# RMS norms of a four-layer trunk: the root and the reciprocal move to 128x2 values with the token on the partition, and TensorE spreads them over PSUM

## The reference, cut to what matters

```python
def rms_norm(x, g):
    x32 = x.astype(jnp.float32)
    y = x32 * lax.rsqrt(jnp.mean(x32 * x32, axis=-1, keepdims=True) + EPS)
    return (y * g.astype(jnp.float32)).astype(x.dtype)

for i in range(DEPTH):                 # 4 layers, the kind of mixer is i mod 3
    h = rms_norm(x, norm_mix[i])
    x = x + mixer(h)                   # 0: attention, 1: RWKV, 2: S5
    h = rms_norm(x, norm_ffn[i])
    x = x + conv_ffn(h, ffn_w_up[i], ffn_conv_w[i], ffn_conv_b[i], ffn_w_down[i])
```

## Time and profile before

| | us |
|---|---|
| Median of 3 runs | 1543.69 (1541.53 to 1544.11) |
| The profiled execution | 1544.98 |
| Its span, first to last instruction | 1543.2 |
| PE busy | 1440.3 (93%) |
| PE weight loads | 1349.6 (87%) |
| DVE busy | 1074.4 (70%) |
| ACT busy | 805.2 (52%) |
| POOL busy | 621.9 (40%) |

### The profile page before, as it was taken

The page is one execution under the profiler, slowest core; times in us unless marked ns, Lnnn a source line. Parts: engine busy times, 40 slices in busy tenths (PEclk is TensorE's granted clock), DMA queues, the critical chain, the costliest instruction groups (busy, mean ns, idle before and its releaser), DMA issues.

```text
span 1543.2 us, 33037 instructions
## 1 busy us (share of the span) xinstructions
PE 1440.3 (93%) x13742; PEld 1349.6 (87%) x13742; DVE 1074.4 (70%) x1604; ACT 805.2 (52%) x1326; POOL 621.9 (40%) x333
## 2 busy tenths in 40 slices
PE   6989999999999888999997767999999899999998
PEld 5988999989887777999987667999989788999988
DVE  6596688743485556888789954798854598597752
ACT  4458575543651334665642334566654458566642
POOL 5232355551005203485542613455554132355553
PEclk9999999999999999999999578999999999999999
DMA  5542455563433001475552003555555442455553
GB/s 163 161 141 83 137 192 181 170 200 104 136 118 128 4 4 56 156 228 186 167 168 80 1 1 100 175 169 187 184 180 169 137 134 87 136 167 189 189 173 103
DMA packets 212055, 210.11 MB, mean 136 GB/s; under 512 B 12098, under 2 KB 211058, under 8 KB 211922
## 3 DMA queue, kind: packets, MB, share of 16 engines
q1 hardware_dynamic: 210784, 206.65, 41.7%
q0 software_dynamic: 800, 1.46, 0.5%
q10 hardware_dynamic: 338, 0.10, 0.0%
HBM read 207.15 MB, written 1.05 MB: 135 GB/s over the span
## 4 chain that ended last, share of the span: by engine, by line
PE 76%; DVE 17%; ACT 4%; issue 2%; ACTq 0%; POOL 0%; DVEq 0%; POOLq 0%
PE psum L406 16%; PE psum L408 15%; PE psum L407 15%; PE psum L759 7%; PE psum L552 5%; PE psum L761 3%; DVE w_low L389 3%; DVE work L2463 2%; PE psum L2391 2%; DVE x_low L506 2%; DVE work L1253 1%; DVE work L501 1%; ACT w_high L381 1%; DVE work L1265 1%; PE psum L1623 1%
## 5 line engine op out<-in xcount | busy, mean ns | idle before, releaser
L389 POOL TENSOR_TENSOR w_low<-ring,w_high 128x1024 fp32r<-128x1024 f32 (+1 forms) x185 | 458.4, 2479 | 747.5 <-ACT w_high L381 713.5
L406 PE MATMUL psum<-x_high,w_high 128*128 128x256 f32 x1856 | 532.4, 287 | 13.3 <-DVE w_low L389 9.7
L407 PE MATMUL psum<-x_low,w_high 128*128 128x256 f32 x1856 | 527.4, 284 | 0.0
L408 PE MATMUL psum<-x_high,w_low 128*128 128x256 f32 x1856 | 527.3, 284 | 0.0
L381 ACT ACTIVATE w_high<-ring 128x1024 fp32r<-128x1024 f32 (+1 forms) x368 | 376.9, 1037 | 226.9 <-PE psum L408 132.8
L389 DVE TENSOR_TENSOR w_low<-ring,w_high 128x1024 fp32r<-128x1024 f32 x183 | 303.4, 1658 | 155.6 <-ACT w_high L381 154.5
L406 PEld LDWEIGHTS psum<-x_high,w_high 128*128 128x128 f32 x1856 | 358.4, 193 | 19.1 <-issue 14.1
L407 PEld LDWEIGHTS psum<-x_low,w_high 128*128 128x128 f32 x1856 | 358.5, 193 | 1.0 <-issue 1.0
L408 PEld LDWEIGHTS psum<-x_high,w_low 128*128 128x128 f32 x1856 | 358.5, 193 | 0.0
L759 PE MATMUL psum<-inner,w_high 128*128 128x512 f32 x528 | 187.0, 399 | 1.4 <-DVE w_low L389 1.4
L870 DVE SCALAR_TENSOR_TENSOR work<-psum,par,work 128x255 f32<-128x255 f32 (+1 forms) x352 | 144.8, 473 | 46.4 <-ACT work L791 46.0
(11 more groups left out here) (325 smaller groups left out, 2201.2 us busy)
## 6 DMA issues: line engine op xcount, KB each, us to landing
ring<-in_ffn_w_up_dram SPq DMA_DIRECT2D x88, 1024.0 KB, 5.1
ring<-in_ffn_w_down_dram SPq DMA_DIRECT2D x32, 1024.0 KB, 5.0
ring<-in_dsa_w_in_dram SPq DMA_DIRECT2D x28, 1024.0 KB, 5.4
ring<-in_ffn_w_down_dram SPq DMA_DIRECT2D x16, 768.0 KB, 4.3
ring<-in_rwkv_w_rkv_dram SPq DMA_DIRECT2D x12, 1024.0 KB, 4.9
ring<-in_dsa_w_out_dram SPq DMA_DIRECT2D x8, 1024.0 KB, 4.9
ring<-in_s_w_glu_dram SPq DMA_DIRECT2D x8, 1024.0 KB, 5.3
ring<-in_rwkv_w_out_dram SPq DMA_DIRECT2D x4, 1024.0 KB, 4.9
```

Source lines behind the costliest of these rows:

```text
L389: eng.tensor_tensor(low, raw, high.bitcast(F32), ALU.subtract).then_inc(sem("w_split", b), 1)
L406: pe.matmul(out_, lhs[0], rhs[0], start=start, stop=False, skip_group_check=True)
L407: pe.matmul(out_, lhs[0], rhs[1], start=False, stop=False, skip_group_check=True)
L408: return pe.matmul(out_, lhs[1], rhs[0], start=False, stop=stop, skip_group_check=True)
```

## The change

The operands of the mean are swapped. The squares are now the stationary operand, 128 tokens at a time, and two columns of mean_all the moving one, so that the mean of a token comes out on the token's partition: `token_means`, two values wide for each of the two blocks of tokens, in bank 7. Root and reciprocal then work on 128x2 values, `token_rs`. `spread_inverse` brings them back: for each block a column of token_rs, broadcast to 128x128, is multiplied with the identity, which leaves 1/root of every token in every partition of bank 7 (`inverse`). DVE scales from there. The six early norms need rstd in SBUF still, and get it by a copy (`tensor_copy`) behind the third chunk. In early norms the spread stands ahead of chunk c = 7 of the first tile. In plain norms the 30 transposes become 6 ahead of the spread and 10 behind.

```diff
--- before.py
+++ after.py
@@ -209,6 +209,7 @@
         sum_head = sb("sum_head", P)
         centre_head = sb("centre_head", P)
         rstd = sb("rstd", T)
+        token_rs = sb("token_rs", TT)
         warm = sb("warm", 2 * DEPTH)
         mu_rest = sb("mu_rest", 6 * DC)
         blocks = sb("blocks", 8, CH)
@@ -462,25 +463,45 @@
             pe.wait_ge(sem("early_split"), DC * h_splits(n) + c + 1)
             if n and c == MEAN_AT:
                 early_mean(pe, n)
+            if c == SPREAD_AT:
+                spread_inverse(pe, n)
 
         def early_mean(pe, n):
 
             pe.wait_ge(sem("squares_added"), 3 * (h_splits(n) + 1))
-            for i in range(2):
-                mm = pe.matmul(banks[7][:, 0:T], mean_all[:, :], sq[n % 2][:, i, :], start=i == 0, stop=i == 1)
+            for b in range(TT):
+                for i in range(2):
+                    mm = pe.matmul(token_means[:, 2 * b:2 * b + 2], sq[n % 2][:, i, b * P:(b + 1) * P], mean_all[:, 0:2],
+                                   start=i == 0, stop=i == 1)
             mm.then_inc(sem("mean_square"), 1)
 
+        token_means = banks[7][:, T:T + 2 * TT]
+        inverse = banks[7][:, 0:T]
+
+        def spread_inverse(pe, n):
+
+            pe.wait_ge(sem("root"), 2 * n + 2)
+            for b in range(TT):
+                mm = pe.matmul(inverse[:, b * P:(b + 1) * P], token_rs[:, b:b + 1].to_broadcast([P, P]), ident[:, :],
+                               start=True, stop=True)
+            mm.then_inc(sem("mean_square"), 1)
+
         MEAN_AT = 4
+        SPREAD_AT = 7
 
         def norm_mean(pe, n):
 
             idle_turns(pe, 22)
-            for c in range(DC):
-                if c % 2 == 0:
-                    pe.wait_ge(sem("squares"), 4 * n + c // 2 + 1)
-                mm = pe.matmul(banks[7][:, 0:T], mean_all[:, :], sq[n % 2][:, c, :], start=c == 0, stop=c == DC - 1)
+            for m in range(4):
+                pe.wait_ge(sem("squares"), 4 * n + m + 1)
+                for b in range(TT):
+                    for c in (2 * m, 2 * m + 1):
+                        mm = pe.matmul(token_means[:, 2 * b:2 * b + 2], sq[n % 2][:, c, b * P:(b + 1) * P],
+                                       mean_all[:, 0:2], start=c == 0 and b == 0, stop=c == DC - 1, skip_group_check=True)
             mm.then_inc(sem("mean_square"), 1)
-            idle_turns(pe, 30)
+            idle_turns(pe, 6)
+            spread_inverse(pe, n)
+            idle_turns(pe, 10)
 
         def idle_turns(pe, n):
 
@@ -489,17 +510,22 @@
 
         def norm_root(act, n):
 
-            act.wait_ge(sem("mean_square"), n + 1)
-            act.activation(rstd[:, :], banks[7][:, 0:T], ACT.Sqrt, bias=eps[:, 0:1]).then_inc(sem("root"), 1)
+            act.wait_ge(sem("mean_square"), 2 * n + 1)
+            act.activation(token_rs[:, :], token_means[:, 0:2 * TT:2], ACT.Sqrt, bias=eps[:, 0:1]).then_inc(sem("root"), 1)
 
         def norm_scale(dve, n, gain, L, then=lambda c: None):
 
-            dve.wait_ge(sem("root"), n + 1)
-            dve.wait_ge(vector_step.sem, vector_step.mark(dve.reciprocal(rstd[:, :], rstd[:, :])))
+            dve.wait_ge(sem("root"), 2 * n + 1)
+            dve.reciprocal(token_rs[:, :], token_rs[:, :]).then_inc(sem("root"), 1)
+            dve.wait_ge(sem("mean_square"), 2 * n + 2)
             for c in range(DC + 1):
                 if c < DC:
                     dve.scalar_tensor_tensor(out=hT[:, c, :], in0=xT[:, c, :], scalar=col(gain, L * DC + c),
-                                             in1=rstd[:, :], op0=ALU.mult, op1=ALU.mult).then_inc(sem("h_ready"), 1)
+                                             in1=inverse, op0=ALU.mult, op1=ALU.mult).then_inc(sem("h_ready"), 1)
+                if c == 2 and splits_h(n):
+                    copied = vector_step.mark(dve.tensor_copy(rstd[:, :], inverse))
+                if c == 5 and splits_h(n):
+                    dve.wait_ge(vector_step.sem, copied)
                 then(c)
                 if c and splits_h(n):
                     dve.wait_ge(sem("h_rounded"), DC * h_splits(n) + c)
```

## The result

The kernel became slower: 1553.19 us in the median of 5 runs (1552.78 to 1557.1), against 1544.11 (1541.53 to 1545.24) of the kernel before in 5 runs, ratio 1.0068, 95% interval 1.0051 to 1.0084. The prediction was 1548.4 with 1544.5 to 1551.8 for its range: the direction is right, the measured time lies outside the range, and the predicted rise of 4.7 is half of the 9.1 that came. The profiled execution took 1555.76 us, 10.8 more than that of before.

What follows compares the result with a forecast made beforehand. Early norms were taken as bound by ACT's wait for TensorE's first tile, then DVE; plain norms by reciprocal latency. Early +4.7, n = 2 +0.2, n = 4 -0.5, start +0.3 gave +4.7: 1543.69 to 1548.4 us, range 1544.5 to 1551.8.

Steps and rivals of the forecast that it cites:

- Early norms: Six early norms: spread 0.43 us on TensorE plus copy 0.35 on DVE lengthen the path, 0.78 each, +4.7 in all.
- The cover: Early norms: two scaled chunks end at 186.0, ahead of the first x_high at 187.5, so the later scaling start costs nothing.
- never idle: Early norm n = 1: from 187.43 to 198.3 us DVE has no idle time and is the path.
- Root, reciprocal, spread: All norms: root 0.27 us instead of 0.48, reciprocal 0.17 instead of 1.75; the spread takes 0.43 of TensorE.
- Scaling from PSUM at no cost: DVE's scalings reading bank 7: 0 us extra, though a skill page's figures gave 4.1 us on 64 scalings.
- Plain norms at full clock: n = 2 and 4: shorter latency from mean to scaling gains 1.1 to 1.2 us each, -2.3 for both.
- The clock: TensorE at plain norms and start: two-column products may drop the granted clock to 0.50, delaying what follows.
- three terms for the clock: +0.2 us at n = 2 (-1.1 to +1.5), -0.5 at n = 4 (-1.1 to +1.0), +0.3 at the start (0 to 1.7).
- The clock stands: Rival, chance 0.27: TensorE's clock does not fall, so 4.7 - 2.3 = +2.4 us, 1546.1, within 0.2%.
- PSUM is dear: Rival, chance 0.06: each DVE scaling from bank 7 costs 0.05 us more, 56 on the path add 2.8: 1551 to 1552.
- faster: Rival, chance 0.06: the reciprocal is on the early norms' path, each gains 0.75 us, 4.5 in all: 1536.9.
- the spread hides: Rival, chance 0.06: early norms' spread and copy fall into existing waits of TensorE and DVE: 1543.5, within 0.2%.

Runs made afterwards that it cites:

- the 16 runs: The changed kernel, unchanged: its first 5 runs (median 1553.19 us) and 11 repeated later (1555.04 us); together mean +8.7 us against the kernel before.
- e2: Changed kernel with 128 columns of mean_all instead of 2 in every norm's mean: 1549.75 us, ratio 1.0012 to the kernel before.
- e9: Changed kernel with 128 columns in both plain norms' means, early means keeping 2: 1549.27 us, ratio 1.0028 to the kernel before.
- e3_off_path: Changed kernel with the spread moved behind the first tile and the rstd copy behind the second scaling: 1548.11 us, ratio 1.0015 to the kernel before.
- e6: Early norms as in the kernel before, plain norms as changed with two-column means: 1552.02 us, ratio 1.0045 to the kernel before.
- e10: Changed kernel with 128 columns in the mean of n = 2 alone: 1550.58 us, ratio 1.0039 to the kernel before.
- e7: Changed kernel with only the rstd copy moved, behind the second scaling: 1548.79 us in a single run.
- e11: Changed kernel with 128 columns in the mean of n = 4 alone: 1552.59 us, ratio 1.0047 to the kernel before.
- e4: Changed kernel with 128 columns in all means, spread behind the first tile and copy behind the second scaling: 1542.88 us, ratio 0.9982 to the kernel before.

## Why the prediction was wrong, by its own steps

- **Early norms.** Right. Taken 0.43 + 0.35 = 0.78 each; measured 0.45 + 0.34 = 0.79 in five of six. n = 0 can't be read so finely, since the low stretches of the start move by more (its stretch read -1.0 to +3.5 over the profiles). The cover held: 1.89 us of DVE's wait were left, where 1.73 were foretold, and ACT's wait was 2.85, where 2.5 to 2.9 were. The reciprocal's 1.75 us bought nothing. That DVE is "never idle" on the path there passes over one step of the chain, an x_high of ACT of 0.43 us, which stands in both kernels and changes nothing in the sum.
- **Root, reciprocal, spread.** 0.26, 0.17 and 0.45 measured, 0.27, 0.17 and 0.43 taken.
- **Scaling from PSUM at no cost.** Right: eight in 3.22 us, against 3.26 from SBUF. The estimate from the Trainium skill's VectorE: DVE Perf Modes (the TRN2 errata, cycle table), 0.065 us more for each, is not what this trace shows.
- **Plain norms at full clock.** Taken -1.1 to -1.2 each; -1.02 and -1.07 measured with two columns, -0.91 and -0.95 with 128. A tenth of a microsecond too hopeful.
- **The clock, the step that failed.** The mechanism was named, its size was not. The forecast has three terms for the clock, all in stretches where narrow products are issued: +0.2 at n = 2, -0.5 at n = 4 (both with the norm's own gain inside) and +0.3 at the start. In their own stretches these came out about right, in part by luck: +1.16, -0.88 and -0.14 in the first profile, +0.53 and -0.68 for the two plain norms in the mean of the five, with single readings from -0.88 to +1.16 at n = 2. What the sum put at nothing is the clock outside these stretches: +1.4 in the first tile of n = 5 in both profiles of the changed kernel, and a part in other stages that no profile pins down. At full clock the eight norms add 4.7 - 2.1 = +2.6; by the prediction's terms the clock was to add 4.7 - 2.4 = +2.3 to that, and two columns cost about 5 (the table). Then 2.6 + 5 = +7.6, near the +8.7 of the 16 runs (two standard errors: 2.2).
- **The rivals.** "The clock stands", at 0.27, is out for the changed kernel. In e2 and e9 the clock does stand at both plain norms; their means are +3.7 and +4.2 where this rival had +2.4, at a mean clock of 0.9644 against 0.9662 of before (two standard errors: 0.0014), a rest of some 1.6 us for which no cause was found. The page that spoke for it, the Trainium skill's TensorE: Matmul & The Clock Gate (the table on why this matters), names idle gaps; by the chain above TensorE's rows follow each other without a break from 374.38 on, and the clock fell at 378.90. "PSUM is dear", "faster" and "the spread hides" are out as the kernel stood; e3_off_path shows that the spread and the copy can be hidden once they are moved.

What stays open: how two columns at n = 2 and n = 4 lower the clock in other stages. Of the 14 profiles, four show a low stretch in the first tile of n = 5 (both of the changed kernel, e6 and e10); three others with a narrow plain mean (e3, e7, e11) don't, and none of the seven without one does. The other stages wander too much from one execution to the next for a single profile to tell: S5 read +1.46 and +0.59 in the two profiles of the changed kernel and -5.86 to +2.09 in the others, narrow and wide alike. More than half of a profile's time at 0.50 lies there, in every profile: 68 us in the mean of the five with two narrow plain means, 61 in that of the seven with none, but the single profiles of each kind scatter by 7 to 8 us about that mean. Layer 0's attention, which lies ahead of both plain norms, was longer by 3.0 to 4.4 also in e2, e4 and e9, whose plain means are wide, so its +3.00 in the first profile is no effect of the plain norms and most likely chance. That the loss follows the width of the plain means is shown by the groups of runs; through which stages it goes beyond 2.5 us is not. Two columns in the early means (e9 against e2) made no difference that these runs can tell: +0.5, two standard errors 2.7. No width between 2 and 128 was run.

## What to carry to other kernels

Before making an operation shorter, look at what its reader waits for last: here 10.5 us of reciprocals in six norms lay beside a wait for TensorE, while 0.45 us on TensorE and 0.34 on DVE lay on the path, and moving both into existing waits made them free. A mean with the token on the partition is cheap, but give its products a wide moving operand: the rows here took 0.11 us at 2 or 128 columns alike, and the wide ones kept the clock at every place, the narrow ones at 2 of 12. Where a time follows the mean granted clock, compare many runs on the same chip: the difference of the means is what a change costs, and the difference at equal clock says how much of it is not the clock.

## What was not expected of the hardware

At 10 of 12 plain means of 2 columns, 32 rows without a gap, the granted clock fell to 0.50 (1.2 of 2.4 GHz) within the mean or right behind it, for 3.4 to 6.8 us; at 12 means of 128 columns at the same pace, and at 4 of 256, it never did. And one kernel, unchanged, spread over 1539.7 to 1556.4 us in 89 runs, with its mean clock (correlation -0.77).
